# Delta rule: the masked key products of a chunk made transposed on VectorE, the row's gate applied when a level's half tile leaves its bank

## The reference

```python
g = jnp.cumsum(g, axis=-1)
decay = exp(where(i >= j, g_i - g_j, -inf))
kk = einsum('bhnid,bhnjd->bhnij', k, k)
m = where(strict, beta_i * kk * decay, 0)
rhs = concatenate([v * beta, k * (beta * exp(g))])
sol = triangular_solve(m, rhs, lower=True, unit_diagonal=True)
u, w = sol[..., :dv], sol[..., dv:]
intra = where(lower_incl, einsum(q, k) * decay, 0)
# then, chunk after chunk:
v_new = u_c - w_c @ state
o = (q_c * exp(g_c)) @ state + intra_c @ v_new
state = state * exp(g_last) + (k_c * exp(g_last - g_c)).T @ v_new
```

## Time and profile before

| | us |
|---|---|
| median of 3 runs (1097.55 to 1097.7) | 1097.55 |
| the profiled execution, its own time | 1097.84 |
| its span in the trace | 1096.5 |
| TensorE busy | 1082.0 (99%) |
| VectorE busy | 537.4 (49%) |
| ScalarE busy | 569.2 (52%) |
| GpSimd busy | 433.8 (40%) |

### The profile page before, as it was taken

One profiled execution on the slowest core, in us unless ns is written; L12 is line 12 of the kernel. 1 busy time (PEld: TensorE's weight loads), 2 busy tenths in 40 slices (PEclk: granted clock), 3 DMA queues, 4 the chain that ended last, 5 costly groups with the idle time before them and its releaser, 6 DMA issues.

```text
span 1096.5 us, 14926 instructions
## 1 busy us (share of the span) xinstructions
PE 1082.0 (99%) x5685; PEld 887.0 (81%) x5685; DVE 537.4 (49%) x1155; ACT 569.2 (52%) x1086; POOL 433.8 (40%) x236
## 2 busy tenths in 40 slices
PE   8999999999999999999999999999999999999997
PEld 7877878778888788888778787789888888888886
DVE  3739789788665224142445455535111115544444
ACT  6556767767677642353556566554222224333333
POOL 4334342342433444553142332345444446444441
PEclk9999999999999999999999999999999999999999
DMA  9133121221322332723222321232333334332312
GB/s 259 47 96 87 44 73 39 78 60 41 93 59 60 94 96 96 232 76 81 78 78 59 96 78 58 77 92 75 105 96 96 96 97 135 99 99 97 100 48 77
DMA packets 140529, 97.24 MB, mean 89 GB/s; under 512 B 9013, under 2 KB 125090, under 8 KB 140458
## 3 DMA queue, kind: packets, MB, share of 16 engines
q1 hardware_dynamic: 138728, 95.03, 29.5%
q10 hardware_dynamic: 1730, 1.25, 0.4%
HBM read 94.14 MB, written 2.91 MB: 89 GB/s over the span
## 4 chain that ended last, share of the span: by engine, by line
PE 95%; ACT 2%; DVE 1%; DMA 1%; issue 0%; POOL 0%; SPq 0%; ACTq 0%; DVEq 0%
PE bank L467 32%; PE bank L1183 14%; PE bank L1201 14%; PE bank L496 6%; PE bank L881 4%; PE bank L855 4%; PE bank L865 4%; PE bank L1214 2%; PE bank L674 1%; PE bank L605 1%; PE bank L617 1%; PE bank L698 1%; PE bank L1029 1%; PE bank L991 1%; PE bank L1011 1%; PE bank L1018 1%
## 5 line engine op out<-in xcount | busy, mean ns | idle before, releaser
L2471 POOL TENSOR_TENSOR ring<-raw_ring,ring 128x1024 fp32r<-128x1024 f32 x160 | 387.3, 2424 | 569.4 <-ACT ring L1227 569.4
L467 PE MATMUL bank<-hT,ring 128*128 128x512 f32 x1536 | 395.0, 402 | 0.5 <-ACT rawsb L1302 0.5
L467 PEld LDWEIGHTS bank<-hT,ring 128*128 128x128 f32 x1536 | 278.0, 188 | 57.6 <-issue 6.5
L1227 ACT CAST ring<-raw_ring 128x1024 fp32r<-128x1024 f32 x160 | 167.3, 1047 | 109.7 <-PE bank L1201 88.9
L1183 PE MATMUL bank<-hT,ring 128*128 128x512 f32 x672 | 152.5, 389 | 0.0
L1201 PE MATMUL bank<-ring,ring_u 128*128 128x512 f32 x672 | 152.5, 389 | 0.0
L1201 PEld LDWEIGHTS bank<-ring,ring_u 128*128 128x128 f32 x672 | 126.1, 188 | 26.2
L1183 PEld LDWEIGHTS bank<-hT,ring 128*128 128x128 f32 x672 | 126.1, 188 | 26.1
L2446 DVE TENSOR_TENSOR ring_u<-u,ring_u 128x1024 fp32r<-128x1024 f32 x32 | 80.7, 2528 | 73.9 <-ACT ring_u L1807 73.9
L2451 DVE TENSOR_TENSOR u<-u 128x512 f32<-128x512 f32 x32 | 22.9, 715 | 139.2 <-ACT u L1814 139.2
L1814 ACT ACTIVATE u<-bank 128x512 f32<-128x512 f32 x32 | 19.1, 598 | 115.3 <-PE bank L1183 108.4
(11 more groups left out here) (292 smaller groups left out, 1476.2 us busy)
## 6 DMA issues: line engine op xcount, KB each, us to landing
raw_ring<-in_w_in SPq DMA_DIRECT2D x144, 256.0 KB, 3.3
raw_ring<-in_w_up SPq DMA_DIRECT2D x64, 256.0 KB, 3.2
raw_ring<-in_w_down SPq DMA_DIRECT2D x64, 256.0 KB, 2.7
raw_ring<-in_w_out SPq DMA_DIRECT2D x32, 256.0 KB, 2.9
x<-in_x SPq DMA_DIRECT2D x8, 512.0 KB, 5.2
raw_ring<-in_w_branch_sb SPq DMA_DIRECT2D x8, 256.0 KB, 2.7
raw_ring<-in_w_branch_gdn SPq DMA_DIRECT2D x8, 256.0 KB, 3.2
cum<-cums SPq DMA_DIRECT2D x4, 512.0 KB, 5.7
```

The lines of the kernel that those rows point to most:

```text
L467: p = pe.matmul(bank, m.slab_k8(n % 4)[:, a, k, :], m.hT[:, b, k, :], start=term == 0, stop=term == 23)
L1227: act.copy(m.ring[:, q, 0, :], m.raw_ring[:, q, :]).then_inc(s.slab_hi[q], 1)
L2471: pool.tensor_tensor(m.ring[:, q, 1, :], m.raw_ring[:, q, :], m.ring[:, q, 0, :].bitcast(F32), ALU.subtract).then_inc(s.slab_lo[q], 1)
```

## The change

The masked product is no longer made and then transposed. K K^T is symmetric, so K K^T times the transposed decay `Ca` is the transposed masked product, except for the gate and norm of its row, which after the transposition belong to a column. VectorE writes it straight to `MT`, behind the transpose of the multipliers. TensorE's four transposes, ScalarE's copy of them and their semaphore go. The missing factor depends on the row of the level's first product alone, so it is applied when that product leaves bank 5: VectorE's `delta_level_y` replaces ScalarE's copy `delta_level`. That is three more VectorE operations of 128x256 a head and four fewer on ScalarE. `delta_ps` counts five steps a head instead of six.

Three orders are written anew. VectorE: `qg` and the level 4 factor stand ahead of row block 2's `stick_soft`; the level 6 factor stands inside the convolution of the key; the level 6 update stands ahead of row block 3's `stick_soft`. TensorE: the levels move against the tile matmuls. GpSimd's order stays; it waits for `gram_set` alone.

```diff
-    def delta_gram_T(i):
-        pe.wait_ge(s.gram_set, 2 * i + 1)
-        for c in range(4):
-            p = pe.transpose(chunk(banks[5], c), chunk(X, c), ident)
-        p.then_inc(s.delta_ps, 1)
...
         tiles.to(50)
-        delta_gram_T(i)
         stick_weights_T(i, 1, 1)
         stick_weights_T(i, 0, 1)
...
         stick_z(i, 2)
-        tiles.to(94)
+        tiles.to(98)
         delta_level_first(i, 4)
-        tiles.to(98)
+        tiles.to(102)
         delta_level_second(i, 4)
-        tiles.to(108)
+        tiles.to(112)
         delta_level_first(i, 5)
-        tiles.to(109)
         stick_weights_T(i, 1, 2)
         stick_weights_T(i, 0, 2)
-        tiles.to(114)
+        tiles.to(117)
         delta_level_second(i, 5)
         stick_z(i, 3)
-        tiles.to(121)
+        tiles.to(124)
         delta_level_first(i, 6)
-        tiles.to(127)
-        tiles.to(135)
+        tiles.to(130)
         delta_level_second(i, 6)
-        tiles.to(144)
+        tiles.to(139)
         delta_solve(i)
         tiles.to(147)
...
-    def delta_mT(i):
-        act.wait_ge(s.delta_ps, 6 * (i + 1))
-        act.copy(MT, banks[5]).then_inc(s.mT_set, 1)
-
-    def delta_level(i, l):
-        w = 1 << l
-        act.wait_ge(s.lev_ps, 6 * i + 2 * (l - 3) - 1)
-        act.copy(by_level(CX[l % 2], l)[:, :, 0, :], banks[5][:, 0:T // 2].rearrange("p (cb w) -> p cb w", w=w)).then_inc(s.lev_y, 1)
...
         for j in range(1, 4):
             dve.wait_ge(s.conv, at + j)
             dve.scalar_tensor_tensor(dst, m.cin[:, n, j:j + T], m.conv_col[:, n, j, i:i + 1], dst, ALU.mult, ALU.add).then_inc(s.conv, 1)
+            if j == 1 and level is not None:
+                delta_level_y(i - 1, level)
...
-        dve.tensor_tensor(X, banks[5], Cb, ALU.mult).then_inc(s.gram_set, 1)
         dve.wait_ge(s.diag, 7 * i + 4)
         dve.transpose(m.multipliers[:, 0:BLOCK - 1, :].rearrange("p k (cs c) -> p k cs c", c=BLOCK),
                       m.diag.rearrange("p (cs k) -> p k cs", k=BLOCK)[:, 0:BLOCK - 1, :].unsqueeze(3)
                       .broadcast_to([P, BLOCK - 1, 8, BLOCK])).then_inc(s.diag, 1)
         dve.wait_ge(s.decay_exp, 3 * i + 3)
-        dve.wait_ge(s.delta_ps, 6 * i + 5)
+        dve.tensor_tensor(MT, banks[5], Ca, ALU.mult).then_inc(s.gram_set, 1)
+        dve.wait_ge(s.delta_ps, 5 * i + 5)
         dve.tensor_tensor(intra, banks[6], Ca, ALU.mult).then_inc(s.gram_set, 1)
...
+    def delta_level_y(i, l):
+        w = 1 << l
+        dve.wait_ge(s.lev_ps, 6 * i + 2 * (l - 3) - 1)
+        row_gate = m.k_stat[:, 4, :].unsqueeze(2).unsqueeze(3).broadcast_to([P, 4, T // (8 * w), w])
+        y = CX[l % 2].rearrange("p (c b two w) -> p c b two w", c=4, two=2, w=w)[:, :, :, 0, :]
+        dve.tensor_tensor(y, banks[5][:, 0:T // 2].rearrange("p (c b w) -> p c b w", c=4, w=w), row_gate, ALU.mult).then_inc(s.lev_y, 1)
...
         least(gate, m.rawg, s.g_sig, 4 * i + 3, s.g_dve)
+        times(qg, qT, misc, s.decay_exp, 3 * i + 1, s.qg)
+        delta_level_y(i, 4)
         stick_soft(i, 2)
         delta_level(i, 4)
-        times(qg, qT, misc, s.decay_exp, 3 * i + 1, s.qg)
         delta_zero(i, 5)
         delta_zero(i, 6)
         times(gate, m.rawg, gate, s.g_sig, 4 * i + 4, s.g_dve)
+        delta_level_y(i, 5)
         stick_gate(i)
         delta_conv(i + 1, 0, qT)
         delta_level(i, 5)
-        delta_conv(i + 1, 1, kT)
+        delta_conv(i + 1, 1, kT, 6)
+        delta_level(i, 6)
         stick_soft(i, 3)
-        delta_level(i, 6)
```

More of the change, by code:

```diff
@@ L279, in __init__ @@
         self.q_sq, self.k_norm, self.k_gate = one("q_sq"), one("k_norm"), one("k_gate")
-        self.gram_set, self.mT_set, self.bk_kd, self.qg = one("gram_set"), one("mT_set"), one("bk_kd"), one("qg")
+        self.gram_set, self.bk_kd, self.qg = one("gram_set"), one("bk_kd"), one("qg")
         self.diag, self.steps = one("diag"), one("steps")
@@ L784, in tensor_program @@
     delta_gram(i)
-    tiles.to(48)
-    delta_gram_T(i)
     tiles.to(100)
@@ L1338, in delta_k_norm @@
         ks = m.k_stat
-        act.wait_ge(s.delta_ps, 6 * i + 1)
+        act.wait_ge(s.delta_ps, 5 * i + 1)
         for c in range(4):
@@ L1467, in scalar_program @@
         stick_exp(i, 1)
-        delta_mT(i)
         tile_a(g + 1)
@@ L1474, in scalar_program @@
         exponential(gate, s.g_dve, 2 * i + 1, s.g_sig)
-        delta_level(i, 4)
         tile_a(g + 3)
@@ L1478, in scalar_program @@
         stick_gate(i)
-        delta_level(i, 5)
         stick_weights(i, 2)
         stick_soft(i, 3)
-        delta_level(i, 6)
         delta_q_log(i + 1)
@@ L1880, in vector_program, with delta_conv @@
     CX = (tmp, PP)
-    def delta_conv(i, n, dst):
+    def delta_conv(i, n, dst, level=None):
         at = 12 * i + 4 * n
         if i:
-            dve.wait_ge((s.delta_ps, s.delta_ps, s.lev_ps)[n], (6 * i - 1, 6 * i - 1, 6 * i - 2)[n])
+            dve.wait_ge((s.delta_ps, s.delta_ps, s.lev_ps)[n], (5 * i, 5 * i, 6 * i - 2)[n])
             if n == 0:
@@ L1955, in delta_decay @@
             dve.wait_ge(s.small_act, 10)
-        dve.wait_ge(s.delta_ps, 6 * i + 2)
+        dve.wait_ge(s.delta_ps, 5 * i + 2)
         for dst, bound, op in ((Cb, m.front, ALU.max), (Ca, m.late, ALU.min)):
@@ L1973, in delta_values @@
     def delta_values(i):
-        dve.wait_ge(s.delta_ps, 6 * i + 3)
+        dve.wait_ge(s.delta_ps, 5 * i + 3)
         dve.wait_ge(s.k_gate, 3 * i + 2)
@@ L1978, in delta_gram @@
     def delta_gram(i):
-        dve.wait_ge(s.delta_ps, 6 * i + 4)
+        dve.wait_ge(s.delta_ps, 5 * i + 4)
         dve.wait_ge(s.decay_in, 2 * i + 2)
@@ L2020, in delta_blocks @@
         dve.wait_ge(s.diag, 7 * i + 7)
-        dve.wait_ge(s.delta_ps, 6 * (i + 1))
         dve.tensor_tensor(whole(X), in_blocks(m.diag_inv), block32, ALU.mult).then_inc(s.inv, 1)
@@ L2172, in vector_program @@
     delta_zero(i, 6)
+    delta_level_y(i, 5)
     delta_level(i, 5)
     merge_least(5)
+    delta_level_y(i, 6)
     stick_soft(i, 2)
@@ L2531, in delta_level @@
         if l == LEVELS[0]:
-            pool.wait_ge(s.mT_set, i + 1)
             pool.wait_ge(s.gram_set, 2 * i + 2)
```

## The result

| | before | after |
|---|---|---|
| median, us | 1097.62 (1097.55 to 1097.7, 4 runs) | 1124.83 (1120.98 to 1127.18, 4 runs) |
| span of the profiled execution, us | 1096.5 | 1122.8 |
| TensorE busy, us | 1082.0 | 1091.6 |

A forecast was written before the change was run, and what follows sets the result against it. TensorE, busy 99% of the span, was taken as the bound, hiding a VectorE with almost no slack. Heads 0 to 2 at +2.4 us each, including the 1.15 gain, and -0.3 in the fourth gave +6.9: 1104.5 us, range 1095.8 to 1111.

The forecast's parts named there:

- The removal: TensorE's transposes L596 and their 0.65 us wait go, so the next group L681 starts 1.15 us earlier, about 84.3.
- The factor's first operation: VectorE's added 128x256 product, estimated from the row of L2031: 0.42 us long, 0.34 of queue time, 1.0 a head.
- The meeting point: Level 4, head 0: GpSimd's split starts at 99.65, 0.55 us ahead of VectorE's first scan, due at 100.2.
- a scan which comes second is stopped: At level 4 the first scan waits for GpSimd's running split and works only from 102.04.
- The turn between the scans: At the last block VectorE was assumed to keep its turn for the second scan; the split then runs 119.7 to 122.1.
- 280.58: Profile row of a GpSimd split taking 2.97 us, read as held through a further VectorE operation, so VectorE keeps its turn.
- the mask behind the split: GpSimd's level 6 mask, some 1.1 us, at level 4; the forecast's sum gave it no turn between the scans.
- rival 1: GpSimd's waiting split or mask goes between the two scans: up to +4.5 us a head, 1110.7 us; chance 0.15.
- 1.55: TensorE, due at 103.8, waits 1.55 us for VectorE's level 4 update and starts level 5 at 105.35.
- The fourth head: Its spacing differs and VectorE waits more there; it was to change the total by -0.3 us.
- its two terms, 0.5 and 0.2: Fourth head: 0.5 us kept as gain for the transposes, 0.2 given back for the later level 5 factor.

The follow-up runs named there:

- experiment 2: Kernel before, with ScalarE's cast and tile copy beside row block 2 put ahead of the level 4 copy in heads 0 to 2: 1100.04 us, ratio 1.0022.
- experiment 3: Changed kernel plus idle TensorE matmuls in heads 0 to 2, 11 ahead of level 5's product, 8 ahead of row block 3's transposes: 1112.31 us, ratio 1.0133.
- experiment 7: Kernel before, with two casts and splits moved ahead into the substitution and the level 6 mask waiting for row block 2's scans: 1103.55 us, ratio 1.0056.

## Why the prediction failed

**The removal: right.** L596 and its wait are gone, and the next group starts at 84.15, where 84.3 was expected; the three tile matmuls ahead of it start at 83.38 instead of 83.51, so it is 1.13 us earlier against them, and 1.15 was worked out. The factor's first operation took 0.42, as the row chosen for it.

**The meeting point: right to a tenth.** The cast was put at 98.5 and is at 98.52, the split at 99.65 and is at 99.63, the first scan at 100.2 and is at 100.04, the level 4 product at 97.9 and is at 97.73. That a scan which comes second is stopped was an assumption; the first scan did stand until the split ended at 101.99. The Trainium skill, SBUF — State Buffer, section Who interferes with whom, has it so (two SBUF inputs against a GpSimd instruction that reads SBUF, the later one fully blocked), and the trace agrees, for scans too.

**The turn between the scans: wrong.** The step is "I assume VectorE keeps its turn for the second scan, as it did at 280.58", and at level 4 the silent assumption that the mask behind the split comes after both scans. Both went the other way, as rival 1 (chance 0.15) had them: TensorE stood 2.64 at level 5, not 1.55, the 1.1 that rival 1 names. The row of 280.58 was misread. Its split and VectorE's next operation are 0.03 apart: it came at the handover, as in experiment 2, and says nothing of a split that has stood for 0.5. The rule quoted above, that whoever issues first holds the pair, read instruction by instruction, gives both turns of after: while the first scan runs, the second is not issued yet, and the split or the mask is. This was in the forecast's own text and was used for the first scan only. The rows set it one limit: asked for 0.03 (before) or some 0.1 us (experiment 2) ahead of the handover, the turn stayed with VectorE.

**The price of a wait: missing,** and the largest term of the miss. The sum has TensorE's waits at their length. At 1.2 GHz behind them the same work takes longer, some 9.6 us in three heads (experiment 3). Neither forecast nor any rival had the term. With the clock kept up the time was 1112.3, near rival 1's 1110.7 (4.9 us a head against its 4.5) and just past the end of the range; with the fall it was 1124.8. The trace of before had no wait of such length in this stretch and showed no fall of the clock, but a forecast that adds waits of 1.5 us and more to an engine that is never idle should have bounded it: doubling the length of a few microseconds of work behind each.

**Adding up.** 1124.83 - 1104.5 = 20.3 us: rival 1 instead of the forecast 6.2 (1110.7 - 1104.5), the clock 9.6, the state's wait L630 2.9, and 1.6 left over. At L630 the split of 135.58 meets a product of VectorE, a third meeting that was not in the forecast:

```profile
136.08 2.43 DVE L1870 SCALAR_TENSOR_TENSOR g<-g,g 128x512 f32<-128x512 f32 x1
```

**The fourth head: right in its sum,** -0.3 forecast, 0.3 given back between the two lines shown first; its two terms, 0.5 and 0.2, were not measured apart.

## What to carry to other kernels

Where two engines exclude each other, place every operation of both on one time line before moving either, and give the turn to the instruction that is already issued when the other ends, if by more than the 0.1 us that left VectorE its turn here: a back-to-back pair of one engine is two turns, with a door between them. An edit that frees ScalarE moves the cast behind it and so GpSimd: here the splits' places were 26.6 of the 27.2 us. And a wait on an engine that is otherwise never idle is priced at its length plus slow work behind it, until a run with the wait filled by idle work says otherwise.

## What the chip showed that was not expected

- Behind waits of 2.64 and 1.96 us TensorE's granted clock fell to its lower level for several us (windows at 0.56 to 0.67), behind another of 2.66 us it stayed at 1.00 (product at once behind it 1.08 us against 1.90). In experiment 7 it fell behind a wait of 1.08 us, and not behind two equal ones. What decides between them is open. Eleven and eight idle matmuls a head kept it at 1.00 and made the kernel 12.5 us faster, 2.9 of them a later wait that fell away. The Trainium skill, TensorE: Matmul & The Clock Gate, section Why this matters for your kernels, warns of idle gaps between bursts of matmuls, behind which TensorE goes back to its lower clock, though of gaps longer than any here. The trace agrees that a gap can lower the clock, and differs on the length: five waits of about 2 to 2.7 us in after and one of 1.08 in experiment 7 were enough.
- Scans lose as other operations with two inputs in SBUF do: two of 128x384 took 4.66 us instead of 1.80 where a split and a mask of GpSimd came between.
- Half a microsecond decides: a split 0.41 behind a product of VectorE cost it nothing (0.68 us), one 0.14 ahead of it made it 2.85. At a handover a tenth may: some 0.1 ahead left VectorE its turn, 0.14 ahead did not.
